# A hybrid decoder layer: the S5 mixer's rotation tables made in the first feed-forward block and kept in DRAM, its matrices made beside another GEMM, and its products in 32-channel row and column tiles

## The reference, cut to what matters

```python
def s5_mixer(u, lambda_re, lambda_im, b_re, b_im, c_re, c_im, d_skip, log_dt):
    ...
    bu_re = jnp.einsum('bsgi,gpi->bsgp', uf, bbar_re)
    bu_im = jnp.einsum('bsgi,gpi->bsgp', uf, bbar_im)
    ...
    _, _, s_re, s_im = lax.associative_scan(combine, (a_re, a_im, bu_re, bu_im), axis=1)
    y = (jnp.einsum('bsgp,gip->bsgi', s_re, c_re.astype(f32))
         - jnp.einsum('bsgp,gip->bsgi', s_im, c_im.astype(f32))
         + d_skip.astype(f32) * uf)
```

## Time and profile before

| what | value |
|---|---|
| median of 3 runs | 2849.67 us (2849.11 to 2850.8) |
| the profiled execution's own time | 2842.94 us |
| its span in the trace | 2840.1 us |
| PE busy | 2545.3 us, 90% of the span |
| DVE busy | 1775.2 us, 63% |
| ACT busy | 992.6 us, 35% |
| POOL busy | 221.9 us, 8% |

### The profile page before, as it was taken

The page is one execution under the profiler, slowest core; times in us unless marked ns, Lnnn a source line. Parts: engine busy times, 40 slices in busy tenths (PEclk is TensorE's granted clock), DMA queues, the critical chain, the costliest instruction groups (busy, mean ns, idle before and its releaser), DMA issues. The chain is left out here.

```text
span 2840.1 us, 39338 instructions
## 1 busy us (share of the span) xinstructions
PE 2545.3 (90%) x16280; PEld 2348.5 (83%) x16280; DVE 1775.2 (63%) x1710; ACT 992.6 (35%) x646; POOL 221.9 (8%) x214
## 2 busy tenths in 40 slices
PE   5689999999999778788999979989799999999897
PEld 5568789887899678788889979989678799777897
DVE  5666667767666548878677775657666545444443
ACT  1044333333333322232334442333334334333333
POOL 0010000560000202232400000000000000000000
PEclk6589999999999879899999999999899999999999
DMA  8767767768677443323356556757476645544552
GB/s 296 270 222 272 260 224 256 276 235 297 213 257 245 149 148 105 104 96 112 119 164 226 204 178 208 237 182 268 150 283 239 220 157 202 172 171 163 161 185 71
DMA packets 293217, 567.64 MB, mean 200 GB/s; under 512 B 9892, under 2 KB 34980, under 8 KB 292324
## 3 DMA queue, kind: packets, MB, share of 16 engines
q1 hardware_dynamic: 292404, 560.32, 57.1%
q0 software_dynamic: 688, 5.51, 0.6%
HBM read 561.59 MB, written 4.19 MB: 199 GB/s over the span
## 5 line engine op out<-in xcount | busy, mean ns | idle before, releaser
L783 DVE TENSOR_TENSOR wlo<-raw,whi 128x2048 fp32r<-128x2048 f32 x400 | 925.2, 2313 | 819.8 <-ACT whi L526 815.3
L526 ACT ACTIVATE whi<-raw 128x2048 fp32r<-128x2048 f32 x400 | 766.2, 1916 | 1337.2 <-PE gps L266 1316.8
L266 PE MATMUL gps<-whi,hs 128*128 128x512 f32 (+1 forms) x2816 | 873.5, 389 | 39.4 <-DVE wlo L783 25.0
L266 PE MATMUL gps<-hs,whi 128*128 128x256 f32 x3584 | 683.4, 293 | 96.9 <-DVE wlo L783 53.2
L266 PEld LDWEIGHTS gps<-hs,whi 128*128 128x128 f32 x3584 | 581.4, 199 | 104.8 <-DVE wlo L783 52.3
L266 PEld LDWEIGHTS gps<-whi,hs 128*128 128x128 f32 x2816 | 532.9, 190 | 144.5 <-DVE wlo L783 27.1
L266 PE MATMUL gps<-wlo,hs 128*128 128x512 f32 (+1 forms) x1408 | 545.0, 387 | 0.0
L266 PE MATMUL gps<-hs,wlo 128*128 128x256 f32 x1792 | 518.6, 289 | 0.0
L266 PE MATMUL gps<-ffs,whi 128*128 128x256 f32 x2752 | 503.9, 286 | 4.7 <-DVE wlo L783 3.5
L266 PEld LDWEIGHTS gps<-ffs,whi 128*128 128x128 f32 x2752 | 432.0, 193 | 9.8 <-DVE wlo L783 6.8
L800 DVE SCALAR_TENSOR_TENSOR acc<-raw,cact,acc 128x512 f32<-128x512 f32 x508 | 383.4, 755 | 15.6
(11 more groups left out here) (222 smaller groups left out, 1537.8 us busy)
## 6 DMA issues: line engine op xcount, KB each, us to landing
raw<-in_w_ffn_in_dram SPq DMA_DIRECT2D x160, 1024.0 KB
raw<-in_w_ada_dram SPq DMA_DIRECT2D x144, 1024.0 KB
raw<-in_w_in_dram SPq DMA_DIRECT2D x80, 1024.0 KB
raw<-in_w_ffn_out_dram SPq DMA_DIRECT2D x56, 1024.0 KB
raw<-in_w_ffn_out_dram SPq DMA_DIRECT2D x40, 768.0 KB
raw<-in_w_a_proj_dram SPq DMA_DIRECT2D x16, 1024.0 KB
raw<-in_w_b_glu_dram SPq DMA_DIRECT2D x32, 512.0 KB
raw<-in_w_out_dram SPq DMA_DIRECT2D x16, 1024.0 KB
```

What stands on the lines that cost most here:

```text
L266: return pe.matmul(out, lhsT, rhs, start=start, stop=stop, skip_group_check=True)
L526: act.activation(whi[:, mpos % SPLIT, :, :], raw[:, pos % RING, :, :], ACT.Copy).then_inc(hi_ready, 1)
L783: dve.tensor_tensor(wlo[:, mpos % SPLIT, :, :], raw[:, pos % RING, :, :], whi[:, mpos % SPLIT, :, :].bitcast(F32), ALU.subtract).then_inc( ...
```

## The change

It does five things.
1. The rotation tables of all 8 blocks are made by POOL right after their factors, in the first feed-forward block, in 16 halves of 128x512 for each table, and stored to a DRAM tensor `rot_kept` (8 MB in all). In the S5 stage they are loaded back, 1 MB for each block, into one of two buffers `tab`.
2. The matrices of all 8 blocks are made during the GEMM "u" instead of beside xbc and z. They are smaller: `maskb` and `pairs` spread B and C over 2 groups instead of 8, so a block has 4 tiles of 128x128 to make (DVE, 4 operations of 128x128), transpose (PE) and copy (ACT, 128x512) where it had 16.
3. B's product reads 32 channels at a time (32 rows of PE, 4 row tiles), C's writes 32 channels at a time (4 column tiles).
4. The two combining adds of the forward rotation leave DVE: C's product now takes four products as they are (`wr`, `wi`, and both tables overwritten in place), with signs folded in, and sums them in PSUM: 16 column-tile products in place of 8 full ones.
5. DVE's scans of a block are in two turns of four instead of one of eight.

```diff
+            for n in range(2 * UT):
+                if n >= 2:
+                    pool.wait_ge(sem(f"rot_stored{n % 2}"), 16 * (n // 2))
...
+                pool.tensor_tensor(sc, big[1], few[1], ALU.mult)
+                tt(cn, big[0], few[0], ALU.mult)
+                tt(cn, cn, sc, ALU.subtract)
+                pool.tensor_tensor(sc, big[0], few[1], ALU.mult)
+                tt(sn_, big[1], few[0], ALU.mult)
+                tt(sn_, sn_, sc, ALU.add)
+                pool.dma_start(rot_kept[n // 2][:, :, 2 * (n % 2):2 * (n % 2) + 2, :], stage[:, n % 2]
+                               ).then_inc(sem(f"rot_stored{n % 2}"), 16)
...
+                if k == 1:
+                    pool.wait_ge(sem("dt_raw"), 1)
+                elif k:
+                    pool.wait_ge(sem("s5_out"), k - 1)
+                pool.dma_start(tab[:, k % 2], rot_kept[k]).then_inc(sem(f"rot_in{k % 2}"), 16)
```

On ACT and DVE, the turns beside the GEMM "u":

```diff
+            def s5_mats():
+
+                for k in range(UT):
+                    act.wait_ge(sem("s5_turned"), k + 1)
+                    act.activation((mats[0] if k < 4 else mats_new)[:, k % 4].rearrange("p m c -> p (m c)"),
+                                   mps[:, k % 2, :], ACT.Copy).then_inc(sem("s5_mats"), 1)
+                    yield
...
+                for k in range(UT):
+                    b = k % 2
+                    if k >= 2:
+                        dve.wait_ge(sem("s5_turned"), k - 1)
+                    for j in range(2):
+                        dve.tensor_tensor(blk[:, b, j, :].rearrange("p (j g i) -> p j g i", j=4, g=2),
...
+                    ins.then_inc(sem("s5_blocks"), 1)
+                    yield
...
                     dve.tensor_tensor(WR, C_, T1, ALU.mult)
-                    dve.tensor_tensor(WI, S_, T2, ALU.mult).then_inc(sem("rot_half"), 1)
+                    dve.scalar_tensor_tensor(out=WI, in0=S_, scalar=-1.0, in1=T2, op0=ALU.mult, op1=ALU.mult
+                                             ).then_inc(sem("rot_half"), 1)
                     dve.wait_ge(sem("rot_half"), one)
-                    dve.tensor_tensor(WR, WR, WI, ALU.subtract).then_inc(sem("s_re"), 1)
-                    yield
                     dve.tensor_tensor(S_, S_, T1, ALU.mult)
-                    dve.tensor_tensor(T2, C_, T2, ALU.mult).then_inc(sem("rot_last"), 1)
-                    dve.wait_ge(sem("rot_last"), one)
-                    dve.wait_ge(sem("s_re"), one)
-                    dve.tensor_tensor(WI, S_, T2, ALU.add).then_inc(sem("rot_rest"), 1)
+                    dve.tensor_tensor(C_, C_, T2, ALU.mult).then_inc(sem("rotated"), 1)
```

On PE:

```diff
+            def s5_mats():
+
+                for k in range(UT):
+                    for _ in range(3):
+                        yield
+                    pe.wait_ge(sem("s5_blocks"), k + 1)
+                    if k >= 2:
+                        pe.wait_ge(sem("s5_mats"), k - 1)
+                    for m in range(4):
+                        ins = pe.transpose(mps[:, k % 2, P * m:P * m + P], blk[:, k % 2, m, :], ident[:, :])
+                    ins.then_inc(sem("s5_turned"), 1)
+                    yield
...
+                        rows_ = slice(32 * j, 32 * j + 32)
+                        ins = mm(pe, mps[:, j, S * rim:S * rim + S], b_t[rows_, rim, :], ub[rows_, k, :], rim == 0, rim == 1)
...
+                    pe.wait_ge(sem("rotated"), k + 1)
+                    c_t = mats[k // 4][:, k % 4]
+                    parts = ((2, wr[:, :, :]), (2, wi[:, :, :]), (3, tab[:, k % 2, 1]), (3, tab[:, k % 2, 0]))
+                    for n, (m, states) in enumerate(parts):
                         for j in range(4):
-                            ins = mm(pe, mps[:, 0, 0:S], ctb[:, rim, j, :], states[:, j, :], rim + j == 0,
-                                     rim == 1 and j == 3)
+                            cols = slice(32 * j, 32 * j + 32)
+                            ins = mm(pe, mps[cols, 0, 0:S], c_t[:, m, cols], states[:, j, :], n == 0, n == 3)
```

More of the change, by code:

```diff
@@ L98, in plan @@
         [("prologue", None), ("norm", 0), ("s5_step", None)] + ffn(1, 0) + [("norm", 1)]
-        + [("gemm", Phase("u", "w_in", OFF_U, NT, 1, "copy", "h", True)),
+        + [("gemm", Phase("u", "w_in", OFF_U, NT, 1, "copy", "h", True, side="mats")),
            ("dt", None), ("s5_begin", None),
@@ L179, in build @@
         wi = at("wi", 12 * K, [P, 4, S])
[L180 to L186, removed]
+        tab = at("tab", W, [P, 2, 2, 4, S])
+        blk = at("blk", R + 40 * K, [P, 2, 4, P])
+        mats = [at("mats0", R + 72 * K, [P, 4, 4, P]), at("mats1", R + 64 * K, [P, 4, 4, P])]
+        mats_new = at("mats_new", R + 32 * K, [P, 4, 4, P])
         Z = R + 64 * K
@@ L195, in build @@
         sp = at("sp", W + 8 * K, [P, 24, ST])
+        stage = at("stage", W, [P, 2, 2, 2, S])
+        rscr = at("rscr", W + 8 * K, [P, 2, S])
         T = R + 80 * K
@@ L737, in _ @@
             todo = list(weights)
-            sides = {"s5": s5(), "ssd": ssd()}
+            sides = {"mats": s5_mats(), "s5": s5(), "ssd": ssd()}
             for kind, ph in steps:
@@ L757, in _ @@
                 elif kind == "dt":
+                    for _ in sides["mats"]:
+                        pass
                     dt_part()
                 elif kind == "s5_begin":
-                    s5_mats(0)
+                    act.wait_ge(sem("s5_blocks"), UT)
+                    act.wait_ge(sem("s5_mats"), UT)
+                    act.activation(mats[1][:, :, :, :].rearrange("p k m c -> p (k m c)"),
+                                   mats_new[:, :, :, :].rearrange("p k m c -> p (k m c)"), ACT.Copy
+                                   ).then_inc(sem("s5_mats"), 1)
                 elif kind == "s5_end":
@@ L1112, in s5 @@
             def s5():
-                C_, S_, T1, T2, WR, WI = (t[:, :, :] for t in (tc, ts, t1, t2, wr, wi))
-                bu = [mps[:, 2 * j:2 * j + 2, :].rearrange("p a (b s) -> p (a b) s", b=2) for j in range(2)]
+                T1, T2, WR, WI = (t[:, :, :] for t in (t1, t2, wr, wi))
+                bu = [mps[:, :, S * j:S * j + S] for j in range(2)]
+                dve.wait_ge(sem("x_saved"), 16)
                 for k in range(UT):
                     one = k + 1
-                    dve.wait_ge(sem("rot_ready"), one)
+                    C_, S_ = tab[:, k % 2, 0], tab[:, k % 2, 1]
+                    dve.wait_ge(sem(f"rot_in{k % 2}"), 16 * (k // 2 + 1))
@@ L1188, in _ @@
                 elif kind == "dt":
+                    for _ in sides["mats"]:
+                        pass
                     dt_part()
-                elif kind == "s5_begin":
-                    s5_blocks(0)
-                    dve.wait_ge(sem("x_saved"), 16)
                 elif kind == "s5_end":
@@ L1506, in _ @@
                 elif kind == "dt":
+                    for _ in sides["mats"]:
+                        pass
                     dt_part()
                 elif kind == "s5_begin":
-                    s5_turn(0)
                     s5_bu(0)
```

115 lines of the change are left out of this document (45 added, 70 removed).

## The result

After the change the kernel takes 2879.48 us (median of 4 runs, 2875.23 to 2881.96), before it 2849.48 us (median of 4, 2849.11 to 2850.8). The ratio is 1.0103, with a 95% interval of 1.0085 to 1.012: slower by 30 us. The forecast was 2845 us, between 2820 and 2878: a small gain was expected, a loss came, and it lies above the upper bound. The ratios in this document compare runs at one level of the granted clock (0.92 to 0.94); the one run that fell to 0.81, of the kernel before beside the first four experiments (2991.36 us), is not in them.

The account below looks back on a forecast made before the run. PE was taken as the bound, busy 2545 of 2840.1 us. The terms 61.5 - 10.8 - 58 + 3 = -4.3 us, on the runs' median of 2849.67 us, gave 2845 us, range 2820 to 2878 us.

Parts of the forecast that it names:

- Part 4: First block: POOL makes there the tables it made beside S5; three bodies at 1 us each, +3 us (0 to 8).
- Rival (d): Stops beside u cost more (85) or POOL disturbs DVE's splits in the first block (+8): 2870 to 2880 us; chance 0.1.
- part 3: S5 stage, seven more blocks: less work for DVE, ACT and PE, with tiled products, -58 us (-33 to -74).
- Part 1: Matrices beside GEMM u: PE stops after slabs 0 to 6 and lower-clock slabs cost +61.5 us (50 to 85).
- "+4" for the last block: End of u, from slab 7 to the dt product: matrices, transposes and ACT's copy stand in between, +4 us (3 to 6).
- Part 2: Start of S5: block 0's matrices, transposes and copies gone, B's product in half the time, -10.8 us (-8 to -12).
- The term that was off is the tiles': S5 products on PE: tiles overlap partly, B's product 1.7 us (0.9 to 3.6), C's 3.5 us (1.8 to 7.2).
- Part 4's loads: S5 stage: table loads of 1 MB have a whole block's time and cost nothing.
- rival (c): S5 products: all four tiles run truly side by side, sum -17.5 us, time 2821 to 2832 us; chance 0.2.

Follow-up runs that it names:

- the first four experiments: Four edits of the changed kernel (e1, e2, e3_ahead, e4), run on one chip with the kernel before, which took 2849.57 us beside them.
- e1: Changed kernel without POOL's table operations of halves 2 to 15, all sixteen stores kept, blocks 1 to 7 using block 0's tables: 2838.2 us, ratio 0.996.
- e4: Changed kernel with POOL's table operations released in groups of three by the count of used slabs, in gaps of DVE: 2836.66 us, ratio 0.9955.
- e7: Changed kernel with POOL's six table operations of each half replaced by twelve memsets, all stores kept: 2832.74 us, ratio 0.9947.
- e2: Changed kernel computing all tables but storing only the first two halves, which every block loads: 2870.11 us, ratio 1.0073.
- e8_one_input: Changed kernel with POOL's six table operations of each half replaced by six operations reading one SBUF input, all stores kept: 2840.24 us, ratio 0.9973.
- e3_ahead: Changed kernel with DVE writing the matrices of blocks 0 and 1 at the end of norm 1, before u: 2826.67 us, ratio 0.9919.

## Why the prediction was wrong, step by step

**Part 4 failed: "+3 us (0 to 8)" was +51.5 us.** It read the earlier trace rows: a body with POOL 87% busy took 47.8 us, the next 47.5, so POOL's work was taken as free. But busy time was the wrong measure. In that body POOL's operations were of 128x32 to 128x256 elements, and the same trace shows their effect in DVE's means: acc 780 ns there and 750 in the next two bodies, splits 2417 and 2292. Splits of before beside growing operations of POOL, DVE first, then POOL:

```profile
606.82 2.33 DVE L783 TENSOR_TENSOR wlo<-raw,whi 128x2048 fp32r<-128x2048 f32 x1
601.21 2.44 DVE L783 TENSOR_TENSOR wlo<-raw,whi 128x2048 fp32r<-128x2048 f32 x1
612.09 2.65 DVE L783 TENSOR_TENSOR wlo<-raw,whi 128x2048 fp32r<-128x2048 f32 x1 [2.94 <-ACT whi L526]
```

```profile
604.86 4.40 POOL L393 TENSOR_TENSOR sp<-sp 128x32 f32<-128x32 f32 x4
600.76 3.16 POOL L393 TENSOR_TENSOR q<-rot,sp 128x128 f32<-128x128 f32 x2
611.95 3.27 POOL L393 TENSOR_TENSOR q<-rot,sp 128x256 f32<-128x256 f32 x2
```

Over the 2.29 us of an undisturbed split that is 0.04 us beside 128x32, 0.15 beside 128x128 and 0.36 beside 128x256 (single rows, read afterwards); beside the table operations of 128x512 it became up to 1.07 (3.36 us). The loss goes by the size of POOL's operation and by how often the two meet, not by POOL's busy time: the four 128x32 took 4.40 us, so POOL itself waited for DVE, and DVE lost next to nothing. An estimate from these rows was within reach: taking twice the 0.36 for twice the size, for 46 DVE operations in the two bodies that became 67.1 us, are 33 us; the operations did grow by 30 times 1.2 us (acc) and 16 times 0.68 (splits), 47 us, and the two bodies got 39 us longer. "The operations are larger" was written down and priced at 1 us for each body. The table operations also read their factors broadcast; no run varies size or pattern alone. Runs e1, e4 and e7 take the loss away by three different roads (no work, work at another time, work that reads nothing), each to within 5 to 10 us of before; e2 shows that 41 of the 51.5 us are there with two of the sixteen stores.

The Trainium skill, page "SBUF — State Buffer", section "Who interferes with whom", states this: a VectorE instruction with two SBUF inputs contends with a GpSimd instruction that reads SBUF, not with one that only writes it. By that rule memsets leave DVE's two-input operations alone, and the trace of e7_fill agrees (751 ns). Section "SBUF: two separate sides" of that page says that whichever of the two starts first has the shared port pair for the whole instruction while the other is blocked. The pairs of after look like that (2.99 us for a table operation of 1.1 us behind a split). The one-input operations of e8_one_input do so only one way: one that meets a running split takes 2.98 us instead of 1.49, but a split that starts at 628.23, 0.14 us after such an operation began, takes 2.62 us, 0.33 more and not 1.35.

**Rival (d)** named POOL's disturbance of the splits, but at +8 us and with a chance of 0.1 shared with another cause; the mechanism was on the list, its size was not worked out from any row. That the measured 2879.48 us lies in (d)'s 2870 to 2880 is luck: the loss was six times its 8 us, and the gain of part 3, larger than forecast, took 11.5 us of it back.

**Part 1 was right: +61.5 forecast, +59.9 measured.** A stop of 5.2 us and 0.76 us until the next slab's first product give 5.96, forecast 5.9. (No row showed its "about 0.1" for semaphore steps; 4.24, 0.1 and 0.9 are 5.24, and the stops measured 5.19 to 5.29.) There are eight, the eighth in place of the "+4" for the last block. Eight times 5.96 are 47.7; the wait before the first dt product shrank by 2.9 (4.36 to 1.44); the 15 us that remain are slabs at the lower clock, forecast 16. The window's clock is 0.74, forecast 0.75. e3_ahead confirms the cause. Matrices of 128x128 take 0.28 us, starts 0.2 apart, as assumed.

**Part 2 was right: -10.8 forecast, -10.7 measured.** Within it two small errors cancelled, which is luck: from the first dt product to block 0's B product it was -8.5 us (8.2 forecast), and B's product went from 5.41 to 2.09 us, of which the stage got 2.2 (2.6 forecast).

**Part 3 had the right parts and a size too small: -58 forecast (-33 to -74), -69.5 measured.** The term that was off is the tiles': "the middle for both: instructions are issued in order and each pair shares one tile, which excludes the full gain". B measured 1.15 us (1.7 taken, 0.9 the bound), C 1.94 (3.5 taken, 1.8 the bound): 2.1 us for each of seven blocks is 15 us on PE, and 11.5 us came. That PE is the floor came near: the last z block takes 33.6 us from unrotation to unrotation (1412.4 to 1446.0), and five slabs with both products are 28.8 + 1.15 + 1.94 = 31.9. The Trainium skill's page "TensorEngine Tiling (Array Packing)", section "Overview", gives up to four times for tiles of 32, and was the better guide: the two products came within 0.25 and 0.14 us of the bounds of 0.9 and 1.8. Section "Tiling Modes" has a change of mode drain the engine; if it does here, it costs no more than these 0.25 and 0.14 us.

**Part 4's loads** of 1 MB were hidden, as forecast: DVE waits for no `tab` that comes from DRAM.

With parts 1 to 3 as they were measured and Part 4 as forecast, the sum would be 59.9 - 10.7 - 69.5 + 3 = -17.3 us, rival (c). With 51.5 in place of the 3 it is +31.2, and +30.0 was measured: the sign turned on this one term.

## What to carry to other kernels

- Work moved to an idle engine isn't free because that engine is idle: ask what both use in the same stretch, and price it by what one operation of the busy engine loses beside an operation of that size, times the number of meetings. Busy time of the other engine does not give that price, and neither does the duration of its operations, which holds its own waiting. A row in which small operations did little harm says nothing about large ones; single operations of the busy engine beside neighbours of growing size do.
- Where an engine waits for another in a fixed rhythm, the gap behind that wait is the place for the third one's work; a wait on a counter that already exists puts it there.
- Small work that a second engine must deliver to the first should not stand behind a large step that itself waits for the first. Here the split ring is two slabs deep, and two steps of lead turned 60 us of loss into 3; one step was not tried.

## What the runs showed of the hardware

- VectorE operations with two SBUF inputs and GpSimd operations with two SBUF inputs of 128x512 take turns: 750 to 1946 ns (128x512) and 2292 to 2975 ns (128x2048) in the mean, while GpSimd's own go from 1.1 to 2.99 us beside a split. Beside GpSimd operations of 128x32, 128x128 and 128x256 a split loses 0.04, 0.15 and 0.36 us.
- GpSimd memsets do nothing to these operations (751 and 2293 ns), one-input operations a little (887 and 2534 ns). VectorE's tensor_scalar of 128x512 with one SBUF input (480 ns alone) is disturbed by all three: 1278 ns, 670 ns beside memsets, 830 ns beside one-input operations.
- An acc operation of VectorE that started while GpSimd issued a store ended only after the next two table operations: 3.05 to 3.06 us instead of 0.75, ten times.
- Four row tiles of 32 run side by side in fp32: 16 instructions of 32x256 in 1.15 us; four column tiles too, 32 instructions of 128x256 in 1.94 us. With eight instructions of one column tile in a row it is 4.60 us.
- Stores of 8 MB in pieces of 512 KB beside the weight slabs (305 GB/s together in e7_fill) leave the first block 4.8 us over before, with memsets on GpSimd; in the kernel after ACT waits no longer for slabs than before (11.1 us, 11.3). That the 10.3 us between the bodies of after and of e2_compute come from the operations of 3.06 us is argued, not tested.
